# Loading x by dimension in halves between the first weight tiles, and the last two expert tiles early

## The reference, cut to what matters

```python
def rmsnorm(x, g):
    xf = x.astype(jnp.float32)
    y = xf * lax.rsqrt(jnp.mean(xf * xf, axis=-1, keepdims=True) + EPS)
    return (y * g.astype(jnp.float32)).astype(x.dtype)

def swiglu_ffn(x, w_gu, w_down):
    gate, up = jnp.split(x @ w_gu, 2, axis=-1)
    return (jax.nn.silu(gate) * up) @ w_down
```

## Time and profile before

| | |
|---|---|
| time, median of 3 runs (range) | 2034.12 us (2033.94 to 2035.27) |
| profiled execution, own time | 2033.76 us |
| its span, first to last instruction | 2032.0 us |
| PE busy | 2015.1 us |
| POOL busy | 1717.0 us |
| ACT busy | 1147.6 us |
| DVE busy | 1050.6 us |
| mean granted TensorE clock | 0.999 |

### The profile page before, as it was taken

How to read it: one execution, slowest core, us unless ns; L and a number is a source line. 1 busy time by engine, 2 the same in 40 slices (tenths; PEclk the granted TensorE clock), 3 DMA queues, 4 the chain that set the end, 5 groups by cost and what they waited for, 6 DMA issues and landing times.

```text
span 2032.0 us, 39053 instructions
## 1 busy us (share of the span) xinstructions
PE 2015.1 (99%) x15622; PEld 1902.5 (94%) x15622; DVE 1050.6 (52%) x1985; ACT 1147.6 (56%) x1952; POOL 1717.0 (85%) x991
## 2 busy tenths in 40 slices
PE   9999999999999999999999999999999999999998
PEld 9999999999999969999889999999999998888886
DVE  6865745555454375224754316996788522222224
ACT  6344874445434485444654545557888655555555
POOL 5999789998999658898766677798777799999997
PEclk9999999999999999999999999999999999999999
DMA  9565456666666524665444454355444456555554
GB/s 350 212 220 191 167 187 247 219 216 250 249 249 227 205 87 150 239 232 205 169 175 145 166 184 180 129 189 173 167 167 167 165 185 204 193 195 193 193 195 147
DMA packets 80756, 395.28 MB, mean 195 GB/s; under 512 B 11100, under 2 KB 12252, under 8 KB 52448
## 3 DMA queue, kind: packets, MB, share of 16 engines
q1 hardware_dynamic: 80608, 393.28, 54.9%
HBM read 392.19 MB, written 1.05 MB: 194 GB/s over the span
## 4 chain that ended last, share of the span: by engine, by line
PE 89%; POOL 5%; DVE 3%; issue 2%; ACT 1%; DMA 0%; SPq 0%; ACTq 0%; POOLq 0%; DVEq 0%
PE bank L543 28%; PE bank L544 27%; PE bank L545 27%; POOL ring_low L496 5%; PE bank L1041 2%; PE bank L2801 1%; PE bank L2802 1%; PE bank L1834 1%; PE bank L1890 0%; ACT ring_high L478 0%; PE bank L1863 0%; DVE ring_low L981 0%; DMA ring_raw<-in_stream 0%; DMA keep_gains<-in_gains 0%; DVE keep_red L2501 0%
## 5 line engine op out<-in xcount | busy, mean ns | idle before, releaser
L496 POOL TENSOR_TENSOR ring_low<-ring_raw,ring_high 128x1024 fp32r<-128x1024 f32 (+1 forms) x408 | 1026.5, 2547 | 190.4 <-ACT ring_high L478 188.6
L2759 POOL TENSOR_TENSOR peerS_low<-peerS_raw,peerS_high 128x512 fp32r<-128x512 f32 x510 | 657.7, 1313 | 88.0 <-ACT peerS_high L2911 85.3
L543 PE MATMUL bank<-keep_xThigh,ring_high 128*128 128x256 f32 x2080 | 581.7, 280 | 0.9 <-DVE keep_xTlow L3092 0.5
L544 PE MATMUL bank<-keep_xTlow,ring_high 128*128 128x256 f32 x2080 | 576.1, 277 | 0.0
L545 PE MATMUL bank<-keep_xThigh,ring_low 128*128 128x256 f32 x2080 | 576.1, 277 | 0.0
L478 ACT ACTIVATE ring_high<-ring_raw 128x2048 fp32r<-128x2048 f32 x204 | 390.2, 1913 | 262.2 <-PE bank L545 242.9
L543 PEld LDWEIGHTS bank<-keep_xThigh,ring_high 128*128 128x128 f32 x2080 | 390.6, 188 | 4.7 <-issue 3.4
L544 PEld LDWEIGHTS bank<-keep_xTlow,ring_high 128*128 128x128 f32 x2080 | 391.6, 188 | 0.3
L545 PEld LDWEIGHTS bank<-keep_xThigh,ring_low 128*128 128x128 f32 x2080 | 390.9, 188 | 0.0
L2911 ACT ACTIVATE peerS_high<-peerS_raw 128x512 fp32r<-128x512 f32 x510 | 320.4, 630 | 115.8 <-PE bank L545 95.8
L543 PE MATMUL bank<-keep_xThigh,peerS_high 128*128 128x256 f32 x1024 | 287.8, 281 | 0.1
(11 more groups left out here) (565 smaller groups left out, 3779.8 us busy)
## 6 DMA issues: line engine op xcount, KB each, us to landing
ring_raw<-in_stream SPq DMA_DIRECT2D x215, 1024.0 KB, 4.8
peerS_raw<-in_experts SPq DMA_DIRECT2D x256, 512.0 KB, 3.8
modcols_w<-in_ada_cols SPq DMA_DIRECT2D x32, 512.0 KB, 5.7
modlate_w<-in_ada_cols SPq DMA_DIRECT2D x8, 512.0 KB, 5.7
modcols_rows<-in_cond_rows SPq DMA_DIRECT2D x3, 1024.0 KB, 6.8
start_x<-in_x SPq DMA_DIRECT2D x2, 512.0 KB, 4.4
ring_raw<-in_stream SPq DMA_DIRECT2D x4, 256.0 KB, 5.5
context_in<-in_ctx SPq DMA_DIRECT2D x1, 1024.0 KB
```

What stands on the lines that cost most here:

```text
L496: self.nc.gpsimd.tensor_tensor(low_[:, cut], self.raw_slot(n)[:, cut], high[:, cut].bitcast(F32), ALU.subtract).then_inc(done.sem, 1)
L543: mm(out, sh, mh, start=start, stop=False)
L544: mm(out, sh, ml, start=False, stop=False)
L2759: g_.tensor_tensor(low[:, m % 2, cut], xraw[:, m % 3, cut], high[:, m % 2, cut].bitcast(F32), ALU.subtract).then_inc(made_low.sem, 1)
```

## The change

x is laid out on the host as the kernel keeps it: `in_x[p, k * 256 + t]`. `start` loads it straight into `self.x`, in two halves of four chunks. No transposes, no `x_in`, no copies from PSUM, and four dummy matmuls fewer. SP's order becomes: tile 0 first half, x first half, gains, tile 0 second half, x second half, tile 1 in two halves, tile 2, ident, tiles 3 to 5, the constants and `cond_rows`, tile 6, and on. ident has a semaphore of its own, which PE waits for before the loop, where `settle_pace` first reads it. ACT and DVE alternate, chunk by chunk, between weights and x for all of tiles 0 and 1. The squares go to PSUM and SBUF by turns, two blocks ahead of tile 2's highs and two behind, and DVE adds them with five additions in place of one reduction.

In `peer`, tiles 254 and 255 get raw places of their own in A's space (`last_raw`), and SP loads them ahead of tile 236. ACT makes the highs of tile 255 after its work on expert group 116 and DVE its lows after `split_low(118)`; both were at the very end.

```diff
@@ start
         @self.block.sync
         def _(sp):
-            sp.dma_start(x_in[:, :, 0:512], x[:, :, 0:512]).then_inc(left.sem, 16)
-            sp.dma_start(x_in[:, :, 512:], x[:, :, 512:]).then_inc(right.sem, 16)
-            sp.dma_start(self.ident, self.dram["ident"]).then_inc(here.sem, 16)
-            sp.dma_start(self.gains, self.dram["gains"].rearrange("p (n k) -> p n k", k=KD)).then_inc(here.sem, 16)
...
-            self.next_load = 1
-            self.loads(sp, self.first)
...
+            piece(0, 0, 2)
+            x_half(0)
+            sp.dma_start(self.gains, self.dram["gains"].rearrange("p (n k) -> p n k", k=KD)).then_inc(self.gained.sem, 16)
+            piece(0, 2, 4)
+            x_half(1)
+            piece(1, 0, 2)
+            piece(1, 2, 4)
+            self.next_load = 2
+            self.loads(sp, 0, end=3)
+            sp.dma_start(self.ident, self.dram["ident"]).then_inc(self.ident_here.sem, 16)
...
-            pe.wait_ge(*here.at(32))
-            pe.wait_ge(*left.at(16))
-            for b in range(KD // 2):
...
-                        last = nc.tensor.transpose(ps[4 + b][:, (k % 2) * T + t * P:(k % 2) * T + (t + 1) * P],
-                                                   x_in[:, t, k * P:(k + 1) * P], self.ident)
-                last.then_inc(self.product_done.sem, 1)
-            for n in range(4):
-                nc.tensor.matmul(ps[0][:, 0:P], self.ones, self.ones, start=True, stop=True)
@@ ffn, tensor
-                        pe.wait_ge(*self.kept.at(1))
                         self.sums_pe(pe, 4)
...
             group(1)
+            if first:
+                pe.wait_ge(*self.ident_here.at(16))
             with pe.Fori(0, TURNS) as turns:
@@ ffn, scalar
+                for k in range(KD):
+                    weights(k // 4, k % 4)
+                    act.wait_ge(*self.x_here[k // 4].at(16))
+                    act.wait_ge(*self.gained.at(16))
+                    s_.activation(self.xT[0][:, k, :], self.x[:, k, :], ACT.Copy, scale=gain[:, k:k + 1]).then_inc(self.xhigh.sem, 1)
...
+                squares(0, 1)
+                for k in range(4):
+                    weights(2, k)
+                squares(2, 3)
@@ ffn, vector
+                for k in range(KD):
+                    weights(k // 4, k % 4)
+                    dve.wait_ge(*self.xhigh.at(k + 1))
+                    v_.scalar_tensor_tensor(self.xT[1][:, k, :], self.x[:, k, :], gain[:, k:k + 1],
+                                            self.xT[0][:, k, :].bitcast(F32), ALU.mult, ALU.subtract).then_inc(self.xlow.sem, 1)
+                for k in range(4):
+                    weights(2, k)
+                half, rest = self.banked(0), sq[:, 6:8, :]
+                dve.wait_ge(*self.squared.at(2))
+                link(v_.tensor_tensor(half, half, sq[:, 2:4, :], ALU.add))
+                dve.wait_ge(*self.squared.at(4))
+                link(v_.tensor_tensor(rest, self.banked(2), rest, ALU.add))
+                v_.tensor_tensor(half[:, 0, :], half[:, 0, :], rest[:, 0, :], ALU.add)
+                link(v_.tensor_tensor(rest[:, 1, :], half[:, 1, :], rest[:, 1, :], ALU.add))
+                v_.tensor_tensor(self.red, half[:, 0, :], rest[:, 1, :], ALU.add).then_inc(self.reduced.sem, 1)
@@ peer, sync
             for m in range(2 * N):
+                if m == 2 * N - 20:
+                    sp.wait_ge(*gal.at(12))
+                    for last in (2 * N - 2, 2 * N - 1):
+                        sp.dma_start(raw_of(last), experts[last % N, :, D:]).then_inc(loaded[3 + last % 2].sem, 16)
+                if m >= 2 * N - 2:
+                    continue
@@ peer, scalar
                 split(N + n + 3, 0)
+                if n == N - 12:
+                    split_last()
@@ peer, vector
                 split_low(n)
+                if n == N - 10:
+                    for h in range(2):
+                        m, cut = 2 * N - 1, slice(h * 512, (h + 1) * 512)
+                        dve.wait_ge(*last_high.at(h + 1))
+                        v_.tensor_tensor(halves_of(m, 1)[:, cut], raw_of(m)[:, cut], halves_of(m, 0)[:, cut].bitcast(F32),
+                                         ALU.subtract).then_inc(last_low.sem, 1)
```

More of the change, by code:

```diff
@@ L721, in start @@
         self.ab_constants()
[L722 to L726 removed]
+        self.gained, self.ident_here, filled, self.first_high, self.first_low = self.counters(
+            "start_gains", "start_ident", "start_filled", "start_high", "start_low")
@@ L735, in _, with piece @@
-            tile = self.dram["stream"][0:1].rearrange("a p n -> p (a n)")
-            for k in range(4):
-                at = slice(k * 512, (k + 1) * 512)
-                sp.dma_start(self.raw_slot(0)[:, at], tile[:, at]).then_inc((self.first_in[k] if k < 3 else self.loaded[0]).sem, 16)
-            self.next_load = 1
-            self.loads(sp, self.first)
+            x = self.dram["x"].rearrange("p (k t) -> p k t", k=KD)
+            def piece(n, a, b):
+                at = slice(a * 512, b * 512)
+                sp.dma_start(self.raw_slot(n)[:, at], self.dram["stream"][n:n + 1].rearrange("a p n -> p (a n)")[:, at]
+                             ).then_inc(self.piece_here(n, a).sem, 16)
@@ L876, in group @@
                 gate_up(i, 1, loop)
-                if i == 1:
+                if i == 1 and not first:
                     pe.wait_ge(*self.kept.at(4))
@@ L970, in _ @@
[L970 to L982 removed]
+                link = Chain(dve, self.dve_chain)
@@ new lines, in weights @@
+                def weights(i, k):
+                    high, low = self.parts(g0 + i)
+                    at = slice(k * 512, (k + 1) * 512)
+                    if k < 3:
+                        dve.wait_ge(*self.first_high.at(3 * i + k + 1))
+                    else:
+                        dve.wait_ge(self.high_done.sem, i + 1)
+                    v_.tensor_tensor(low[:, at], self.raw_slot(g0 + i)[:, at], high[:, at].bitcast(F32), ALU.subtract
+                                     ).then_inc((self.first_low if k < 3 else self.low_done).sem, 1)
@@ L1019, in _ @@
                 beside.vector_columns(dve)
-        self.end_update()
+        if first:
+            self.xhigh.base += KD
+            self.xlow.base += KD
+            self.squared.base += 3
+        else:
+            self.end_update()
         self.end_sums()
@@ L3406, in layout @@
     return dict(
[L3407 removed]
+        x=cols_block(x[0].T, 0, T), stream=stream, experts=experts, ident=np.eye(P, dtype=np.float32), gains=gains,
         ab_taps=taps, ab_cols=rgb, ab_if=ml_if, ab_b=ml_b, ab_mask=ml_mask, ab_sel=ml_sel,
```

101 lines of the change are left out of this document (35 added, 66 removed).

## The result

| | before | changed |
|---|---|---|
| median (range) | 2033.88 us (22 runs) | 2036.49 us (22 runs) |
| ratio, 95% interval | 1 | 1.002 (1.0014 to 1.0025) |
| profiled execution, span | 2032.0 us | 2035.1 us |
| first real product | 9.68 | 7.47 |
| sum of squares | 24.74 | 23.09 |

What follows compares the result with a forecast made beforehand. It took TensorE to be the bound, busy 2015.1 of 2032.0 us. Start -2.7, with 0 for POOL, sums and loads, end and pace, took 2034.12 to 2031.4 us; 80% range 2029.8 to 2033.2.

Steps and rivals of the forecast that it cites:

- SyncE two loads of 512 KB, which push tile 236 back by up to 2.5 us once: Near the end: the early loads delay tile 236 once, making POOL begin late by 0.4 to 1.3 us with added work.
- so 1.0 us of delay hides: At the end: POOL's last low, made at 2017.21 and due at 2018.2, can slip 1.0 us without holding PE.
- End: 0, bounds -0.76 and +0.3: At the kernel's end: the early load and splits change the time by 0 us, between -0.76 and +0.3.
- DVE two lows of 0.68 to 1.5: Near the end: the last tile's two lows, made early, take DVE 0.68 to 1.5 us each.
- Rival F: At the start: PE, idle 1.5 us after the dummies, runs slow again and loses 1.5 us, 2032.9; chance 0.02.
- E: In the loop: the slow pace lasts on through the next stage, costing 5.1 less 2.7, 2036.5 us; chance 0.05.
- B: At the first loop turn: the slow pace ends at the new wait, another 1.3 us gained, 2030.1; chance 0.16.
- I take a landing at 6.0: At the start: the gains land at 6.0 us, bounds 5.2 and 6.39, which puts the first product at 7.0.
- Both are faster than PE ... no stall: After the first product: ACT and DVE prepare chunks faster than PE's 1.36 us each; slack 0.7 us, no stall.
- Leaves what PE waits for: At the end: the change leaves PE's 0.6 us wait for `GA3low`, with its product 0.76 us late.
- D: At the end: the early load moves POOL past DVE's operation, 0.76 us more gained, 2030.7; chance 0.09.

Runs made afterwards that it cites:

- e2: The end part of the change alone (early loads, highs and lows of the last tile), with the old start: 2036.66 us, ratio 1.0016 to the kernel before.
- e1: The start part of the change alone, with the old `peer`: 2033.32 us, ratio 0.9996 to the kernel before.
- e4: Changed kernel with the last tile's highs and lows put back to the end, the early loads left together: 2035.6 us, ratio 1.001 to before.
- e3: Changed kernel with the two early loads apart, tile 254 behind 236 and 255 behind 240: 2034.24 us, ratio 1.0006 to before.
- e10: e3 with DVE's two lows of the last tile apart, at experts N-10 and N-7: 2033.17 us, ratio 0.9997 to before.
- e5: Changed kernel with the mends of e3 and e4 together, loads apart and highs and lows late: 2032.62 us, ratio 1.0 to before.
- e8: e5 with A's last group `GA3` split six experts earlier on ACT and DVE: 2031.55 us, ratio 0.9992 to before.
- e11: e8 with PE waiting for tile 2's lows chunk by chunk, not for all four at once: 2031.95 us, ratio 0.9991 to before.
- e12: The kernel of e8 run again on another occasion: 2031.77 us, ratio 0.9988 to before.
- e6: e5 with ACT's highs of the last tile early again, only DVE's lows late: 2032.28 us, ratio 0.9994 to before.
- e7: e1 with a quarter of tile 0 and a quarter of x loaded ahead of all: 2034.23 us, ratio 1.0004 to before.
- e9: e8 with 20 instead of 12 dummy matmuls before the first product: 2033.11 us, ratio 1.0002 to before.

## Why the prediction was wrong

**The failed step is the end: "SyncE two loads of 512 KB, which push tile 236 back by up to 2.5 us once", with "so 1.0 us of delay hides" and "End: 0, bounds -0.76 and +0.3".** It measured +7.6 us in the profile of the changed kernel and +4.0 in that of e2; in the medians it is +2.7 (e2) to +3.3 (the changed kernel over e1). Three things went wrong in it.

1. *The DMA delay was named and not followed.* Tile 236 came 8.07 us after its issue, 4.5 beyond the usual 3.6. The prediction priced the push at up to 2.5, turned it into a lateness of POOL of 0.4 to 1.3, and let that hide in the slack of the very last low. POOL in fact stood idle for 3.34 us, and PE needed that tile's low, and the A low of the same group behind the same landing, at group 108, where 6.2 us from issue to ACT was all that fitted. What was beyond it reached PE in full (0.44, 1.68 and 1.88 us in e2, e4 and the changed kernel; none in e3, where tile 236 goes first).
2. *The slack was read in the wrong place.* "DVE two lows of 0.68 to 1.5" would have been 3.0 at its upper end, and they took 3.23. The slack of 1.0 us was that of POOL's last low, at the end. The one that counted was that of DVE's A low at expert 118: DVE idles 2.05 us in each cycle of 2.72, so two operations that together take 3.2 can't fit in one cycle, and e10 shows that one nearly can. The rows also say how long such an operation takes: of the 128 A lows of the kernel before, 127 begin inside an operation of POOL, and each ends 0.28 to 0.29 us behind it, be it after 0.68 us or after 1.51; the extra 128x512 lows end 0.55 behind. The Trainium skill, page "SBUF — State Buffer", section "SBUF: two separate sides", states the exclusive lock on the ports that DVE and POOL share, which the prediction cited for the third's low. This trace agrees with it in those ends. The prediction applied it to the one wait that existed and not to the operations it added.
3. *The end had no term for the clock.* Behind each of the two waits of this execution the granted clock went to its lower level, which added 1.6 us to 1.9. Rival F had this mechanism, for the start alone, with a chance of 0.02. It is not in every execution: the waits of e2 and e4 had nothing of it.

**Rivals.** None of them had this: E, the slower one, was a matter of pace. Its number, 2036.5, is the measured median by accident: the slow pace ended at the first turn at the latest in the changed kernel's profile. B was seen there (32.85 us for the first turn), but the new start alone doesn't decide it: the turn took 32.8 to 32.9 in e5, e8, e11 and e12 and 34.1 in e1, e3, e4, e6, e7, e9 and e10, all with the new start. F was seen in e6 and e7, not in the changed kernel.

**The start: right in mechanism, over-sized.** "I take a landing at 6.0" measured 6.3 to 6.4 on ACT, the upper bound; high and low of the first chunk took 0.51 and 0.48, not 0.42 and 0.44. First product: 7.47 instead of 7.0, 0.07 beyond its bound, and 7.5 to 8.0 in the other runs that load and begin in the same way. "Both are faster than PE ... no stall" missed the wait for all four lows of tile 2, 0.39 for 0.11. High of tile 3 at 18.67 instead of 17.6, because tile 1's first half came at 10.80 instead of 9.9. First down product 30.35 instead of 29.6, with no wait on POOL, as forecast, by 0.2 us instead of 0.5. What reaches the loop is 1.5 us (e1) and not 2.7; the medians show 0.65, with an interval that holds both.

**The old wait.** "Leaves what PE waits for" was right: 0.58 in the changed kernel. D's price for it, 0.76, is what e8 and e12 got back by another way (0.8 to 0.9), and e11 and e9 in part or not at all.

What stays open: what sets the pace of 113 or 118 ns per product from one execution to the next, worth 1.3 us per turn, and whether the new start makes the fast one more frequent (the two profiles with the old start have 34.1); why the same three loads brought tile 236 to ACT after 6.6 us in e2 and 7.9 and 8.1 elsewhere; when a wait of PE is followed by the low clock; and why down to end varies by 1.3 us between profiles with the same end (e8, e9, e11, e12).

## What to carry to other kernels

A load that is brought forward "into idle time" is put in front of another load: price the next tile's landing, then walk down the program of the engine that waits for it, list what stands behind, and ask when TensorE needs each of them. Before adding work to an engine with 75% idle time, compare the addition, at its contended duration, with the idle time of one cycle, and spread it if it doesn't fit. A wait of TensorE of about 2 us can cost 1.6 more by the clock, in some executions and not in others; and an earlier first product is worth only what the loads behind it can follow. Last, one profile is one execution: its 7.6 us stood for some 3 in the medians.

## What the runs showed of the hardware

- Idle TensorE of 1.88, 1.90, 2.36 (e3), 2.27 (e6) and 2.06 us (e7) was each time followed by a stretch of 3.4 us with a granted clock of 0.5; 0.93 (changed kernel), 1.49 (e8) and 1.56 us (e12) before the first product were not. Not always, though: 2.82 us in e2 and 1.68 in e4 left the clock at full.
- The same 24 dummy matmuls took 4.47, 4.59, 5.46 and 5.49 us in four executions: their distance goes from 213 to 110 ns at some point that moves. In each trace that shows the change the clock record begins there, with the full level: at 4.30 us before, where the distance changes at 4.37, and at 4.55 in e6 (4.60). In the changed kernel it begins at 6.38, and all its dummies, the last of them at 6.14, are 213 apart. So the slow ones fit the lower level.
- A VectorE subtraction of two SBUF inputs that began inside one of GpSimd's ended 0.28 us (128x256) or 0.55 us (128x512) behind it. So while the two alternated, VectorE's 128x512 took 1.51 to 1.80 us and GpSimd's 1.29 to 1.71, against 0.64 (two in 1.28) and 1.28.
- Behind two more loads of 512 KB a third of the same size took 6.6 to 8.1 us from issue to the engine that waited for it; in the kernel before the same load landed after 3.1.
